# Final layer norm of a mixture-of-experts layer: token lists for each expert group, one tile per expert unit

## The chip, the cores and the metric

The kernel runs on one core of a Trainium2 chip. The metric is the device time of one execution in microseconds (us). The core has five engines with their own instruction queues: TensorE (PE, matmuls), VectorE (DVE), ScalarE (ACT), GpSimd (POOL) and SyncE (SP, which here only starts DMAs). Each engine runs its instructions in order; they wait for each other through semaphores. POOL also starts all indirect DMAs, those that gather or scatter rows by an index list.

## The reference, cut to what matters

```python
x = layer_norm(ALPHA * x + fourier_mixer(x), ln_g[0], ln_b[0])      # h, (4096, 1024) float32
scores = sigmoid(x @ w_router)                                      # 32 experts in 4 groups of 8
sel = scores + b_router
group = argmax(sum of the two highest sel of each group)            # one group per token
experts = the two highest sel inside that group
gate = scores[experts] / sum
y[t] = sum_k gate[t, k] * (silu(x[t] @ w_gate[e]) * (x[t] @ w_up[e])) @ w_down[e]
out = layer_norm(ALPHA * x + y, ln_g[1], ln_b[1])
```

Both experts of a token lie in the same group. So the sum of a token is complete when the last expert of its group is done.

## The kernel before, in words

The first stage is a two-step Fourier transform and two projections; it ends with the first layer norm, whose rows h are stored twice in DRAM: in h_rows, from which the experts gather, and in sums (`acc`), into which they add. The norm is invariant to scale, so ALPHA is divided out of the gates and the epsilon. Beside it the router runs for 256 tokens a group of steps (`choose`, `take_ranks`, `place`): it ranks every token within its experts by matmuls with a triangular matrix, keeps the counts in `base`, and POOL writes an entry (token, gate) of 8 bytes for each of the two experts into `lists` (`list_tokens`, L1543, four indirect DMAs). An expert's list is laid out over 64 lanes.

The expert stage runs over units: 320 entries of one expert. A unit with more than 256 entries is wide, else narrow. The number of units and which expert and rows each has come from a table `utab` that DVE works out from the counts between L1370 and L1400. With the inputs of the reference there are 33 units. All matmuls are float32 made of three passes over a high and a low part. In a unit (the functions `unit` of each engine)

- SP loads twelve pieces of weights of 512 KB, four each of gate, up and down (`load_piece`, L566), into six slots. A slot is free when DVE has split what was in it. Ahead of piece 4 it waits for `ent_ok` and loads the list entries of the next unit.
- ACT rounds each piece to its high part, DVE subtracts to get the low part (`split`, L1056 and L1356).
- TensorE runs four blocks of gate products, then four of up products in two banks (`first_products`, L880): block k of the up products from the third on needs `hid_ok` of block k - 2. Then four blocks of down products (`down`, L893) with the transposes of the next unit's rows between them, and in a wide unit the third product `down_c`.
- ACT applies silu to the gate blocks. For each block k DVE multiplies (hid), ACT rounds it (hidT high), DVE subtracts (hidT low).
- ACT and DVE each scale half of the y rows; POOL adds them to `sums` by indirect DMA with addition (`scatter`), the second tile only after the first has landed. In a wide unit a third scatter follows.
- POOL also gathers the rows of the unit after the next, waits for all of it, and copies the entries one step on (`ent_now`, `ent_next`).

DVE's order in unit u is: four splits of down pieces of u; for each k the split of piece k of u + 1 (k < 3), hid(k) and the low part; two transposed tiles; hidC; splits and tiles of u + 1 with the two y halves between them. ACT's order follows the same pattern. POOL's iteration u begins with the wait for the first y rows of u, as its scatters, gathers and waits for u - 1 have come first.

The final stage begins when POOL has seen the last scatter land (`moe_done`). It goes over 32 tiles of 128 consecutive rows in eight buffers: SP loads, DVE takes the statistics (`statistics`, L1213) and inverts, ACT takes the root and normalises, DVE multiplies by the gain, POOL adds the shift (L1687), SP stores.

## Time and profile before

| | us |
|---|---|
| median of 3 runs | 2350.23 (2346.81 to 2350.3) |
| the profiled execution | 2350.37 |
| its span, first to last instruction | 2348.4 |
| expert stage, first gate product of the first unit to that of the last | 860.6 to 2173.6 |
| from the landing of the last scatter to the end | 2219.0 to 2348.4 |

The page has the busy time and share of each engine, a timeline in 40 slices, and the costliest groups of instructions. A row of the timeline names the start, the duration, the engine, the line, the operation, and output<-input by the program's names; in brackets stands how long the engine sat idle before it and what released it. TensorE's clock has two levels, 1.2 and 2.4 GHz; the profile gives the granted one as 0.5 and 1.

### The profile page before, as it was taken

To read this page: it belongs to the slowest core of one execution; us is meant where nothing else is said; L and a number is where in the kernel's file an instruction comes from. 1 tells how busy PE (TensorE), PEld (TensorE's weight loads), DVE (VectorE), ACT (ScalarE), POOL (GpSimd) and SP (SyncE) were. 2 spreads that over 40 slices of the span, in tenths; PEclk is the share of its full clock that TensorE was granted. 3 is DMA by queue.
4 is the path that set the end of the run, shared out by engine and by line. 5 is a ranking of instruction groups with operands and counts; after the bars stand their busy time and mean duration, and the time that the engine had idled before them with its cause. 6 is when DMAs were issued, how large, how long until landed. Compare 5 with 4: busy or idle time off the path is not lost.

```text
span 2348.4 us, 37687 instructions
## 1 busy us (share of the span) xinstructions
PE 2127.3 (91%) x12222; PEld 1801.6 (77%) x12223; DVE 1373.1 (58%) x2254; ACT 998.2 (43%) x1442; POOL 582.7 (25%) x493
## 2 busy tenths in 40 slices
PE   8999899999999449999999999999999999999600
PEld 3443678888888349999999999999999999998500
DVE  3321148888887746555655656555555565555298
ACT  1221123333233226555555645655455565554143
POOL 1000034444544411211121121212111121211166
PEclk9999999999999769999999999999999999999855
DMA  6880233443333347767776866877677777766376
GB/s 226 283 287 21 67 126 113 147 147 125 116 127 108 126 153 210 222 203 195 219 216 184 248 194 211 227 223 197 180 220 218 219 218 228 209 202 183 98 286 238
DMA packets 136067, 435.59 MB, mean 185 GB/s; under 512 B 30912, under 2 KB 35008, under 8 KB 131904
## 3 DMA queue, kind: packets, MB, share of 16 engines
q1 hardware_dynamic: 98592, 307.12, 38.6%
q0 software_dynamic: 37440, 128.01, 21.6%
q8 instruction: 21, 0.34, 0.1%
q14 instruction: 14, 0.11, 0.0%
HBM read 328.01 MB, written 108.10 MB: 186 GB/s over the span
## 4 chain that ended last, share of the span: by engine, by line
PE 90%; POOL 3%; issue 3%; DMA 2%; DVE 2%; ACT 0%; SPq 0%; POOLq 0%; ACTq 0%; DVEq 0%
PE ps L877 36%; PE ps L901 15%; PE ps L759 15%; PE ps L696 5%; POOL fin_r L1689 3%; PE ps L865 3%; PE ps L741 3%; PE ps L909 2%; PE ps L715 2%; PE ps L793 2%; PE ps L650 1%; PE ps L780 1%; PE ps L700 1%; PE ps L870 1%; PE ps L659 1%
## 5 line engine op out<-in xcount | busy, mean ns | idle before, releaser
L901 PE MATMUL ps<-wd_hi,hidT 128*128 128x512 f32 x1056 | 293.0, 402 | 0.4 <-ACT hidT L1099 0.4
L1359 DVE TENSOR_TENSOR wd_lo<-wraw,wd_hi 128x1024 fp32r<-128x1024 f32 x132 | 161.9, 1226 | 199.0 <-ACT wd_hi L1057 198.7
L901 PEld LDWEIGHTS ps<-wd_hi,hidT 128*128 128x128 f32 x1056 | 190.1, 189 | 36.3 <-ACT hidT L1099 0.8
L1359 DVE TENSOR_TENSOR wg_lo<-wraw,wg_hi 128x1024 fp32r<-128x1024 f32 x132 | 161.4, 1224 | 92.6 <-ACT wg_hi L1057 92.5
L1632 POOL DMA_INDIRECT sums<-yrow_a,ent_now x33 | 57.2, 1733 | 558.4 <-DVE yrow_a L1422 515.4
L1359 DVE TENSOR_TENSOR wu_lo<-wraw,wu_hi 128x1024 fp32r<-128x1024 f32 x132 | 160.7, 1218 | 52.0 <-ACT wu_hi L1057 51.9
L877 PE MATMUL ps<-mxT_hi,wg_hi 128*128 128x256 f32 (+1 forms) x1056 | 163.3, 297 | 13.4 <-issue 13.4
L1099 ACT CAST hidT<-hid 128x320 fp32r<-128x320 f32 x132 | 60.7, 460 | 257.3 <-DVE hid L1440 257.3
L877 PEld LDWEIGHTS ps<-mxT_hi,wg_hi 128*128 128x128 f32 x1056 | 149.7, 191 | 17.9 <-issue 16.0
L877 PE MATMUL ps<-mxT_lo,wg_hi 128*128 128x256 f32 (+1 forms) x1056 | 163.2, 297 | 0.0
L877 PE MATMUL ps<-mxT_hi,wg_lo 128*128 128x256 f32 (+1 forms) x1056 | 162.6, 297 | 0.0
L877 PE MATMUL ps<-mxT_hi,wu_lo 128*128 128x256 f32 (+1 forms) x1056 | 162.0, 296 | 0.0
L877 PE MATMUL ps<-mxT_hi,wu_hi 128*128 128x256 f32 (+1 forms) x1056 | 161.8, 296 | 0.0
L877 PE MATMUL ps<-mxT_lo,wu_hi 128*128 128x256 f32 (+1 forms) x1056 | 161.8, 296 | 0.0
L1057 ACT CAST wu_hi<-wraw 128x1024 fp32r<-128x1024 f32 x132 | 135.8, 1054 | 36.6 <-DMA wraw<-expert_w_up 31.8
L877 PEld LDWEIGHTS ps<-mxT_lo,wg_hi 128*128 128x128 f32 x1056 | 149.3, 192 | 0.0
L877 PEld LDWEIGHTS ps<-mxT_hi,wg_lo 128*128 128x128 f32 x1056 | 148.7, 191 | 0.0
L877 PEld LDWEIGHTS ps<-mxT_lo,wu_hi 128*128 128x128 f32 x1056 | 147.9, 190 | 0.0
L877 PEld LDWEIGHTS ps<-mxT_hi,wu_hi 128*128 128x128 f32 x1056 | 147.9, 190 | 0.0
L877 PEld LDWEIGHTS ps<-mxT_hi,wu_lo 128*128 128x128 f32 x1056 | 147.9, 190 | 0.0
L1005 ACT CAST xt_hi<-ps 128x256 fp32r<-128x256 f32 x128 | 41.4, 375 | 246.9 <-PE ps L741 246.9
L901 PE MATMUL ps<-wd_lo,hidT 128*128 128x512 f32 x528 | 142.3, 391 | 0.0
(212 smaller groups left out, 4120.0 us busy)
## 6 DMA issues: line engine op xcount, KB each, us to landing
wraw<-expert_w_gate SPq DMA_DIRECT2D x132, 512.0 KB, 5.4
wraw<-expert_w_up SPq DMA_DIRECT2D x132, 512.0 KB, 5.4
wraw<-expert_w_down SPq DMA_DIRECT2D x132, 512.0 KB, 4.4
xch<-x SPq DMA_DIRECT2D x16, 1024.0 KB, 6.7
first_stage<-ych SPq DMA_DIRECT2D x16, 1024.0 KB, 8.3
yt<-first_stage SPq DMA_DIRECT2D x16, 1024.0 KB, 4.9
fin_r<-sums SPq DMA_DIRECT2D x32, 512.0 KB, 3.9
out<-fin_r SPq DMA_DIRECT2D x32, 512.0 KB, 2.9
```

The source lines that it names most:

```text
L696: mm = nc.tensor.matmul(dst, foldT[:, m, g, c * P:(c + 1) * P], T[:, m, g, h * HALF:(h + 1) * HALF], start=(g == 0), stop=(m == 1 and g == ...
L715: nc.tensor.matmul(bank[s1_bank(n)], f1, xch[:, b, n % 4 // 2, n % 2 * HALF:(n % 2 + 1) * HALF], start=True, stop=True).then_inc(job_ps, 1)
L741: mm = nc.tensor.matmul(s2_bank(jj)[:, lo:lo + P], yt[:, b, q, cc * P:(cc + 1) * P], m2t[:, b, q, :], start=True, stop=True)
L759: mm = nc.tensor.matmul(ps[:, cols], xt[l][:, m, c, :], w[r][:, c, cols], start=(n == 0 and c == 0 and not edge_row), stop=(n == 2 and c = ...
L865: mm = nc.tensor.transpose(psT[k % 2][:, lo:lo + P], xrow_s[t][:, c, :], ident)
L877: mm = nc.tensor.matmul(ps[k % 2][:, 0:n], w[l][:, c, k * P:(k + 1) * P], mxT[r][:, c, 0:n], start=(i == c == 0), stop=(i == 2 and c == CH ...
L901: mm = nc.tensor.matmul(psY[h], hidT[:, l, c, t * P:(t + 1) * P], wd[r][:, c, cols], start=(i == c == 0), stop=(i == 2 and c == FC - 1))
L1057: nc.scalar.copy(piece(0, j), wraw[:, j % SLOTS, :]).then_inc(whi_ok, 1)
L1099: nc.scalar.copy(hidT[:, 0, k, :], hid[:, k % 2, :]).then_inc(hh_ev, 1)
L1359: nc.vector.tensor_tensor(piece(1, j), wraw[:, j % SLOTS, :], piece(0, j).bitcast(F32), ALU.subtract).then_inc(wlo_ok, 1)
L1632: pool.indirect_dma_start(acc, bass.IndirectOffsetOnAxis(ap=ent_now[0:n, t, 0:1], axis=0), yrow[t], None, compute_op=ALU.add).then_inc(don ...
L1689: nc.gpsimd.tensor_tensor(fin_r[:, b, :], fin_r[:, b, :], lnb2, ALU.add).then_inc(fh_ok, 1)
```

## The change

The final normalisation is spread over the expert stage.

- Each of the 4 expert groups gets a token list too. `LISTS` is 36; a list is now linear, 35 x 128 entries, so that lanes and their bit operations go. A third entry per token (without a gate) is written by `list_tokens`: six indirect DMAs instead of four. The padding entries of the expert lists point to 512 spare rows of `sums` and `h_rows`, which are filled from x (before: 128); those of the group lists to real tokens.
- `ln_table` on DVE, with one turn over TensorE, works out `ltab`: for each unit u which tile of 128 tokens it normalises, among those whose group was finished before u, one new one a unit. Where none is ready, the unit repeats the last (at first tile 0, whose sums are not final; it is done again later). It also has the start of each tile in the lists and the number of batches of ten that remain.
- In unit u POOL first gathers the tile's rows from `sums` (`ln_gather`), DVE, ACT, DVE normalise them at the places shown below, and POOL scatters them to `out` between its two y scatters (`ln_store`). At the end of its iteration POOL waits for that store. SP waits for it ahead of loading the next tile's token numbers, which come between weight pieces 9 and 10.
- After the units the remaining tiles are done in batches of ten (`FB`), gathered and scattered by POOL; the shift moves from POOL to DVE. Each store waits until the one before it has landed.
- The entries of a unit are loaded by three DMAs instead of four; the gain and shift vectors are loaded ahead of the expert stage.

The diff, cut to its core:

```diff
-UROWS = UNIT // LANES
-LROWS = 2 * S // LANES
-USED_ROWS = S // LANES + 2
+LISTS = E + EG
+CAP = 35 * P
+FILL = 512
 STARTS = -(-S // UNIT)
-LANE_BITS = LANES.bit_length() - 1
-LIST_BITS = (E * LROWS).bit_length() - 1
 MAX_UNITS = 2 * S // UNIT + E
 SLOTS = 6
 PIECES, GU_PIECES = 12, 8
-FB = 8
+FB = 10
...
-            sp.wait_ge(pad_made, 1)
-            sp.dma_start(lists.rearrange("(p e r) w -> p e (r w)", p=LANES, e=E)[:, :, 0:2 * USED_ROWS],
-                         bass.AP(padl.tensor, padl.offset,
-                                 [list(padl.ap[0]), [0, E], [1, 2 * USED_ROWS]])).then_inc(pad_out, 16)
-            sp.dma_start(acc[S:S + P, :], x[0:P, :]).then_inc(pad_out, 16)
-            sp.dma_start(hd[S:S + P, :], x[0:P, :]).then_inc(pad_out, 16)
+            sp.wait_ge(pad_made, 4)
+            lists_pad = lists.rearrange("(e p r) w -> p e (r w)", p=P, e=LISTS)
+            for pad, lo, hi in ((padl[0], 0, E), (padl[1], E, LISTS)):
+                sp.dma_start(lists_pad[:, lo:hi, :],
+                             bass.AP(pad.tensor, pad.offset,
+                                     [list(pad.ap[0]), [0, hi - lo], [1, 2 * CAP // P]])).then_inc(pad_out, 16)
+            sp.dma_start(acc[S:S + FILL, :], x[0:FILL, :]).then_inc(pad_out, 16)
+            sp.dma_start(hd[S:S + FILL, :], x[0:FILL, :]).then_inc(pad_out, 16)
...
+            sp.dma_start(lng2, bcast(ln_g[1], P)).then_inc(ln2_in, 16)
+            sp.dma_start(lnb2, bcast(ln_b[1], P)).then_inc(ln2_in, 16)
+            sp.wait_ge(ltab_ok, 1)
+            own_wait(sp, glist_out, 32 * GROUPS, sp_gate)
+            load_ln_tile(ln_slot(0))
...
+                    if j == 9:
+
+                        tile = ln_slot(u)
+                        own_wait(sp, lrow_out, 16 * u, sp_gate)
+                        load_ln_tile(tile)
...
+            first_tile = sp.value_load(ltab[:, LANES + LN_COLS + 1:LANES + LN_COLS + 2], min_val=0, max_val=MAX_LN)
+            with sp.Fori(0, batches(sp)) as i:
+                own_wait(sp, batch_ok, i + 1, sp_gate)
                 for b in range(FB):
...
+                    start = ln_start(sp, first_tile + FB * i + b)
+                    sp.dma_start(lents[:, b, :], lists[ds(start, P), :]).then_inc(lents_in, 16)
+            own_wait(sp, batch_ok, batches(sp) + 1, sp_gate)
...
+            def ln_deviation(u):
+                act.wait_ge(lvar_ok, u + 1)
+                nc.scalar.activation(lnstd[:, 0:1], lnmv[:, 0, 1:2], ACT.Sqrt, bias=eps2_c).then_inc(lstd_ok, 1)
+
+            def ln_normal(u):
+                act.wait_ge(lsh_ok, u + 1)
+                nc.scalar.activation(lnrow, lnrow, ACT.Identity, bias=lnsh[:, 0:1], scale=lnrs[:, 0:1]
+                                     ).then_inc(lnorm_ok, 1)
...
                         split(u + 1, k)
                     act.wait_ge(hid_ok, 4 * u + k + 1)
                     nc.scalar.copy(hidT[:, 0, k, :], hid[:, k % 2, :]).then_inc(hh_ev, 1)
+                    if k == 0:
+                        ln_deviation(u)
+                    if k == 1:
+                        ln_normal(u)
...
+            def ln_table():
+                link(nc.vector.tensor_scalar(gti, base[:, E:LISTS], float(P - 1), None, ALU.add))
+                link(nc.vector.tensor_scalar(gti, gti, P.bit_length() - 1, None, ALU.logical_shift_right))
+                nc.vector.tensor_scalar(lim, base[:, E:LISTS], float(-P), 0.0, ALU.add, ALU.max)
+                link(nc.vector.tensor_copy(tiles, gti))
+                nc.vector.tensor_scalar(ends, ucum.rearrange("p (g j) -> p g j", j=EPG)[:, :, EPG - 1], unit_c,
+                                        None, ALU.is_le)
+                link(nc.vector.tensor_tensor_scan(upto, tiles, zer[:, 0:EG], 0.0, ALU.add, ALU.add))
+                link(nc.vector.tensor_tensor(ends, ends, tiles, ALU.mult))
+                link(nc.vector.tensor_tensor(past, upto, tiles, ALU.subtract))
+                nc.vector.tensor_reduce(lcol[:, 0:1], ends, AX, ALU.add)
+                nc.vector.tensor_scalar(lcol[:, 2:3], upto[:, EG - 1:EG], -1.0, unit_c, ALU.add, ALU.min)
...
+                nc.vector.tensor_reduce(lcol[:, 1:2], pick, AX, ALU.add).then_inc(lcol_made, 1)
+                dve.wait_ge(ltab_ps, 1)
+                done, last_u, steps_f, more_f = lrow_f
+                link(nc.vector.tensor_tensor_scan(done, ones[0:1, 0:LANES], psLtab[:, 0:LANES], 0.0,
+                                                  ALU.add, ALU.min))
...
+            LN_STEPS = 2
+
+            def ln_statistics(u):
+                dve.wait_ge(lrow_in, 16 * u + 16)
+                step.begin(unit_steps + LN_STEPS * u)
+                statistics(lnrow, 0).then_inc(lvar_ok, 1)
+
+            def ln_invert(u):
+                dve.wait_ge(lstd_ok, u + 1)
+                link(nc.vector.reciprocal(lnrs[:, 0:1], lnstd[:, 0:1]))
+                nc.vector.scalar_tensor_tensor(lnsh[:, 0:1], lnmv[:, 0, 0:1], -1.0, lnrs[:, 0:1],
+                                               ALU.mult, ALU.mult).then_inc(lsh_ok, 1)
+
+            def ln_gain(u):
+                dve.wait_ge(lnorm_ok, u + 1)
+                nc.vector.tensor_tensor(lnrow, lnrow, lng2, ALU.mult).then_inc(lgain_ok, 1)
+
+            def ln_shift(u):
+                dve.wait_ge(lgain_ok, u + 1)
+                nc.vector.tensor_tensor(lnrow, lnrow, lnb2, ALU.add).then_inc(lfin_ok, 1)
+
             def unit(u, more):
                 wide = unit_wide(dve, u)
                 for k in range(FC):
                     split(u, GU_PIECES + k)
+                ln_statistics(u)
                 for k in range(FC):
                     if more and k < FC - 1:
                         split(u + 1, k)
+                    if k == 1:
+                        ln_invert(u)
+                    if k == 3:
+                        ln_gain(u)
                     dve.wait_ge(u_ps, 4 * u + k + 1)
                     dve.wait_ge(silu_ok, 4 * u + k + 1)
                     nc.vector.tensor_tensor(hid[:, k % 2, :], sgate[:, k, :], psU[k % 2][:, 0:UNIT],
@@ -1445,6 +1549,7 @@
                 if more:
                     turn_x(u + 1, 0)
                     turn_x(u + 1, 1)
+                ln_shift(u)
...
+                nc.vector.tensor_tensor(fin_r[:, b, :], fin_r[:, b, :], lng2, ALU.mult).then_inc(fb_ok, 1)
+                dve.wait_ge(fb_ok, t + 1)
+                nc.vector.tensor_tensor(fin_r[:, b, :], fin_r[:, b, :], lnb2, ALU.add).then_inc(fh_ok, 1)
+
+            with dve.Fori(0, batches(dve)) as i:
+                for b in range(FB + 2):
+                    if b < FB:
+                        normal(FB * i + b, i, b)
+                    if 0 < b <= FB:
+                        invert(FB * i + b - 1, (b - 1) % LB)
+                    if b >= 2:
+                        gain(FB * i + b - 2, b - 2)
...
-                for s in range(2):
-                    for k in range(2):
+                for k in range(3):
+                    for s in range(2):
+                        j = 3 * s + k
                         pool.indirect_dma_start(
-                            lists, bass.IndirectOffsetOnAxis(ap=desti[:, 2 * s + k:2 * s + k + 1], axis=0),
-                            payg[:, 4 * s + 2 * k:4 * s + 2 * k + 2], None).then_inc(list_out, 16)
+                            lists, bass.IndirectOffsetOnAxis(ap=desti[:, j:j + 1], axis=0),
+                            payg[:, 2 * j:2 * j + 2], None).then_inc(list_out if k < 2 else glist_out, 16)

             def shift(g, b):
...
+            def ln_gather(u):
+                own_wait(pool, lent_in, 16 * u + 16, pool_gate)
+                pool.indirect_dma_start(lnrow, None, acc, bass.IndirectOffsetOnAxis(ap=lent[:, 0:1], axis=0)
+                                        ).then_inc(lrow_in, 16)
+
+            def ln_store(u):
+                own_wait(pool, lfin_ok, u + 1, pool_gate)
+                pool.indirect_dma_start(out, bass.IndirectOffsetOnAxis(ap=lent[:, 0:1], axis=0), lnrow, None
+                                        ).then_inc(lrow_out, 16)
+
             def unit(u, ahead):
                 wide = unit_wide(pool, u)
+                ln_gather(u)
                 for t in range(2):
                     pool.wait_ge(ya_ok, 2 * u + t + 3)
                     own_wait(pool, yd_ok, 2 * u + t + 3, pool_gate)
                     if t:
                         own_wait(pool, y_out, 32 * u + 16, pool_gate)
                     scatter(t, P, y_out)
+                    if t == 0:
+                        ln_store(u)
                 if ahead == 2:
                     turned(u + 1)
                     gather(u + 2)
...
+                own_wait(pool, lrow_out, 16 * u + 16, pool_gate)
...
+            with pool.Fori(0, batches(pool)) as i:
+                own_wait(pool, lents_in, 16 * FB * i + 16 * FB, pool_gate)
                 for b in range(FB):
-                    fin(FB * i + b, b)
+                    pool.indirect_dma_start(fin_r[:, b, :], None, acc,
+                                            bass.IndirectOffsetOnAxis(ap=lents[:, b, 0:1], axis=0)
+                                            ).then_inc(fin_in[b], 16)
+                for b in range(FB):
+                    if b:
+                        own_wait(pool, fin_out, 16 * FB * i + 16 * b, pool_gate)
+                    own_wait(pool, fh_ok, FB * i + b + 1, pool_gate)
+                    pool.indirect_dma_start(out, bass.IndirectOffsetOnAxis(ap=lents[:, b, 0:1], axis=0),
+                                            fin_r[:, b, :], None).then_inc(fin_out, 16)
+                own_wait(pool, fin_out, 16 * FB * i + 16 * FB, batch_ok)
```

## Rows read from the trace of the kernel before

**Rows 1.** The page, busy us of each engine, share of the span, instructions.

```profile
PE 2127.3 (91%) x12222; PEld 1801.6 (77%) x12223; DVE 1373.1 (58%) x2254; ACT 998.2 (43%) x1442; POOL 582.7 (25%) x493
```

**Rows 2.** Windows: us, busy PE, PEld, DVE, ACT, POOL; clock, DMA share, GB/s.

```profile
860.60:2173.60 1313.00, 1309.73 (x8576) 1228.03 (x8576) 750.97 (x912) 711.86 (x974) 239.05 (x220) 1.00 0.72 209
1470.51:1506.36 35.85, 35.85 (x259) 33.85 (x258) 22.27 (x28) 21.42 (x30) 6.75 (x6) 1.00 0.78 234
2219.30:2348.40 129.10, 0.00 (x0) 0.00 (x0) 111.14 (x192) 48.97 (x64) 74.98 (x32) 0.50 0.74 268
```

**Rows 3.** DMA issues of POOL: count, median us from issue to landing.

```profile
xrow_a<-h_rows,ent_in POOLq DMA_INDIRECT x33, 8.0
...
sums<-yrow_a,ent_now POOLq DMA_INDIRECT x33, 8.3
...
rows<-x,rowg POOLq DMA_INDIRECT x32, 5.0
h_rows<-rows,rowg POOLq DMA_INDIRECT x32, 3.8
```

**Rows 4.** Timeline of the final stage: start, us, engine, line, operation.

```profile
2240.88 0.29 ACT L1139 ACTIVATE lnstd<-lnmv,eps_c 128x1 f32<-128x1 f32 x1 [1.44 <-DVE lnmv L1218]
...
2242.80 0.68 DVE L1215 BATCH_NORM_STATS2 lnst<-fin_r 128x6 f32<-128x512 f32 x1
2242.95 2.35 POOL L1689 TENSOR_TENSOR fin_r<-fin_r,lnb 128x1024 f32<-128x1024 f32 x1 [1.23 <-DVE fin_r L1495]
...
2244.22 0.21 DVE L1218 BATCH_NORM_AGGREGATE lnmv<-lnst 128x2 f32<-128x12 f32 x1
...
2245.24 1.21 DVE L1495 TENSOR_TENSOR fin_r<-fin_r,lng 128x1024 f32<-128x1024 f32 x1
2245.35 1.24 ACT L1144 ACTIVATE fin_r<-fin_r,lnsh,lnrs 128x1024 f32<-128x1024 f32 x1 [0.60 <-DVE lnsh L1484]
```

**Rows 5.** Timeline of POOL around two narrow units, and of SP.

```profile
1466.23 1.75 POOL L1632 DMA_INDIRECT sums<-yrow_a,ent_now  x1 [13.90 <-DVE yrow_a L1422]
1475.29 1.56 POOL L1632 DMA_INDIRECT sums<-yrow_b,ent_now  x1 [7.31 <-DMA sums<-yrow_a,ent_now]
...
1487.27 0.91 POOL L1661 COPY ent_next<-ent_in 128x6 int32<-128x6 int32 x1 [2.28 <-DMA xrow_b<-h_rows,ent_in]
...
1525.30 0.19 POOL L1661 COPY ent_next<-ent_in 128x6 int32<-128x6 int32 x1 [4.71 <-DMA xrow_c<-h_rows,ent_in]
...
1488.42 1.46 SPq L561 DMA_DIRECT2D ent_in<-expert_lists  x2
```

**Rows 6.** Chain in order of time: gate and up products of units.

```profile
1470.51 23.04 PE ps L877 x192
...
1952.20 28.16 PE ps L877 x192
```

**Rows 7.** Timeline of DVE, then ACT, in the narrow unit from 1470.51.

```profile
1484.94 0.49 DVE L1440 TENSOR_TENSOR hid<-sgate,ps 128x320 f32<-128x320 f32 x1 [0.25 <-PE ps L877]
...
1486.90 1.23 DVE L1359 TENSOR_TENSOR wg_lo<-wraw,wg_hi 128x1024 fp32r<-128x1024 f32 x1 [0.46 <-ACT wg_hi L1057]
1488.05 0.48 DVE L1440 TENSOR_TENSOR hid<-sgate,ps 128x320 f32<-128x320 f32 x1
...
1471.19 1.28 ACT L1057 ACT_TABLE_LOAD   x1 [0.40 <-issue]
1472.48 1.05 ACT L1057 CAST wd_hi<-wraw 128x1024 fp32r<-128x1024 f32 x1
...
1494.11 0.46 ACT L1099 CAST hidT<-hid 128x320 fp32r<-128x320 f32 x1 [1.04 <-DVE hid L1440]
```

**Rows 8.** Timeline of PE, first matmuls of the expert stage.

```profile
860.61 2.07 PE L877 MATMUL ps<-mxT_hi,wg_hi 128*128 128x256 f32 x8 [10.08 <-issue]
```

**Rows 9.** Chain in order of time: the last unit's scatters.

```profile
2206.19 6.04 DMA sums<-yrow_a,ent_now
...
2213.01 5.97 DMA sums<-yrow_b,ent_now
```

More of the change, by code:

```diff
@@ L240, in trunk_kernel @@
         ucol = at("ucol", 152.5, 8)
+        gt = [at(f"gt{i}", 156 + i / 32, EG) for i in range(7)]
+        gti = at("gti", 156.5, EG, I32)
+        lcol = at("lcol", 156.75, 4)
+        lrow_f = [at(f"lrow_f{i}", 157 + i / 4, LANES)[0:1, :] for i in range(4)]
         grow = Row(192, 200)
@@ L852, in _ @@
             mm.then_inc(utab_ps, 1)
+            pe.wait_ge(lcol_made, 1)
+            for k in range(2):
+                mm = nc.tensor.matmul(psLtab[:, k * P:(k + 1) * P], lcol[:, k:k + 1], ident,
+                                      start=True, stop=True)
+            mm.then_inc(ltab_ps, 1)
             pe.sem_inc(y1_ps, 2)
```

238 lines of the change are left out of this document (121 added, 117 removed).

## Prediction

> **What bounds the kernel now.** I read the page's engine shares first [rows 1]: TensorE is busy 91% of the span; VectorE (DVE), ScalarE (ACT) and GpSimd (POOL) are at 58, 43 and 25%. The table by stage [rows 2] then shows two regimes. In the expert stage (860.6 to 2173.6 us, 32 units, 41.03 us each) TensorE runs all but without a gap at full clock, 35.85 us for a narrow unit. The final normalisation, from 2219.3 on, has no TensorE work at all. So 129 us of tail are to be won, and every microsecond that the new work adds to a unit is paid 32 times. The third view is the order on each engine inside one unit [rows 5 to 7], because every engine takes its instructions strictly in order.
>
> **How much leaves the tail.** The routing follows from the reference's inputs alone: the four groups hold 992, 1017, 1033 and 1054 tokens, 8+8+9+9 = 34 tiles of 128 rows, and there are 33 units (as many scatters in [rows 3]), 16 of them wide. The first eight units repeat tile 0, the other 25 do one tile each, 9 remain: one batch of 10. In the tail now a tile costs 3.57 us, POOL's shift of 2.35 and DVE's gain of 1.21 in turn [rows 4]. Afterwards, from the landing of the last scatter: ten list loads, which SP issues at 0.73 each [rows 5], and about 2 to land, 9.3; first gather, with its issue, 5.4: 14.7; then on DVE three statistics at 1.65, two inverts at 0.35, one gain and one shift at 1.21 before the first tile is out, 23. Then 4.45 a tile (1.65 + 0.35 + 2.42), the last two without statistics, 60; a last store of 5, in all 65. The stores are a serial chain too: with the 3.8 us of the h_rows stores [rows 3] plus issue it keeps up with DVE, with the 8.3 of the scatters the tail would take 109. I take 65, because these are plain writes like the first. Before, this stretch took 2348.4 - 2219.0 = 129.4 [rows 9]. **Gain 64**, at worst 20.
>
> **What it costs in a unit: DVE waits for a gather that is sent late.** The new statistics stand on DVE between the four splits of the down weights and the first hidden product, hid(0), and wait for the row gather of the same unit. That gather is the first instruction of POOL's iteration. Where is POOL then? The narrow unit starts on TensorE at 1470.51 [rows 6]. POOL sends the previous unit's first scatter at 1466.23 and its second when that has landed, at 1475.29; the gathers for a later unit follow, and the iteration ends with the copy of ent_next at 1487.27, 16.8 us into the unit; the next one at 1525.30 is 18.9 into its unit [rows 5]. These are the last two of eleven units read this way, 16.1 to 19.0, mean 17.6. But hid(0) was due at 1484.94, +14.4 [rows 7]. So the new gather is sent after the product that it now holds up.
> The landing L of that gather: 17.6, + 0.7 because the scatters come later relative to the next unit (below), + 0.8 for copy, semaphores and loop, + the gather itself. Its price lies between 5.0 (rows from x, little else in flight) and 8.0 (xrow_a) [rows 3]; I take 6.5, because weight loads go out at the same time, though fewer than beside xrow_a. L = 25.6 us after the unit's start. From L: statistics 1.65 [rows 4], the split behind them 1.2 and hid(0) 0.49 [rows 7]: it ends at H0 = 28.9.
> TensorE needs hid(0) out of the bank for its third up product, at +17.3 in a narrow unit (three quarters of the 23.04 us [rows 6]): it stands for 11.6 us, in a wide one for 7.7. What is late next, counted from H0 with the durations of [rows 4, 7]: ACT casts hid (0.5), loads the square root's table (1.28), takes the root (0.29) and casts a weight (1.05), 3.0; DVE splits it, inverts and forms hid(1), 5.1 (3.1 in the trace). ACT cast 0.5, normalisation 1.24, weight cast, DVE split and hid(2), 9.4. ACT cast, DVE low half, gain 1.21, hid(3), 12.05; its cast, 12.6. The down products need that. From the same cast to the next unit's start it was 11.8 (1494.57 [rows 7] to 1506.36 [rows 2]), less 0.6 for matmuls that are already done: the next unit starts at H0 + 23.8. The shift (1.21) ahead of hidC hides behind the down products; but the first y rows are ready only 4.5 instead of 5.1 before the next unit, which is the 0.7 above.
> A narrow unit thus takes 28.9 + 23.8 = 52.7, +16.85. Wide ones, half of the units, lose less: their longer gate and up products (28.16 against 23.04 [rows 6]) hide in the wait, 2.56 on average. (16.85 - 2.56) x 32 = **457**. In the first unit POOL has nothing ahead of the gather and is early, so only the longer chain counts, about 3 instead of 17: -14. The last unit, to its first scatter: +9.
>
> **TensorE's clock.** After the stop of 10.08 us ahead of the stage the first eight matmuls ran at 1.2 GHz and took 2.07 us [rows 8]; later eight of them take 0.96 (23.04 / 24). Each unit now has such a stop and a shorter one ahead of the down products. The slow stretch after the first lies inside the chain to hid(1), that after the second may not. I take 1 us a unit, +33; bounds 0 and 3, that is 0 and +99.
> The Trainium skill, "TensorE: Matmul & The Clock Gate", section "Why this matters for your kernels", asks for no idle gaps over about 3 us between bursts of matmuls, or the clock falls to half. The row agrees; by that rule both stops of every unit would be punished, which is rival (c).
>
> **The table load.** In the trace a load takes 1.28 and the next cast starts right behind it [rows 7]; that is what I counted. The Trainium skill, "ScalarE: Activation LUTs", section "What ACT_TABLE_LOAD costs", gives 1.38 us of draining beside it. By that another 1.4 x 33 = 46 us would be lost; the rows show no such gap, and they decide.
>
> **The rest.** DMA: a gather and a store of 0.5 MB each join a narrow unit whose DMA engines are 78% busy [rows 2], but the unit gets half as long again, so no bound there. POOL's store goes out while POOL waits for its first scatter: nothing. SP now waits for that store ahead of down pieces 10 and 11, which come about 11 us into the unit instead of before it; queued behind are the next unit's gate weights, which DVE wants only after L. The stop itself hides this; without it, it would cost 2 to 4 us a unit. List tables: about 35 linked operations of 0.2 [rows 4] and a turn over TensorE, 8 us, most of it in DVE's idle time ahead of the first transposes: +3, bounds 0 and +10. First stage: 3.3 MB more to fill, 12 us at the tail's 268 GB/s [rows 2], in a queue ahead of loads of x: +4, bounds 0 and +15. Routing: two more small list DMAs per group on POOL, which is not the bound, and one DVE step fewer: 0, bounds -5 and +10.
> Sum: 2350.4 (the profiled execution; its span is 2348.4, the median of the runs shown 2350.2) + 457 - 14 + 9 + 33 + 3 + 4 - 64 = 2778, **about 2780**.
>
> **Rivals.** (a) The latencies fall, because the unit is longer. The last unit shows undisturbed scatters: 6.8 us to the second and 6.0 to land [rows 9], instead of 9.1 and some 9. POOL would be 3.3 earlier and the gather take 5.0: 32 x 4.8 = 154 less, 2626. For it: the queues are quiet while all engines wait; against: the delayed pieces and four gate pieces now go out beside these very scatters.
> (b) The wait is covered and only the order costs. If the gather landed by +11, hid(0) would be in time; but 23.8 behind it instead of 21 costs a narrow unit 3 and a wide one about 1: +65 + 7 - 64, 2358. POOL would have to be 14 us earlier than in all eleven units.
> (c) Both stops halve the clock: the down products of every unit partly at 1.2 GHz, 3 us a unit instead of 1: 2846.
> (d) The other side: the gather is covered and the chain fits beside TensorE's products, so that the tail's gain is left: 2350 + 7 - 64 = 2293. One point decides: whether DVE's wait ahead of hid(0) ends before +11. POOL's rows speak against it.
>
> **How the numbers follow.** Forecast 0.66; (a) 0.16; (c) 0.10; (b) 0.03; (d) 0.05. The forecast's own bounds (gather -48 or +48, clock -33 or +66, tail stores up to +44, the rest up to +28) make 2690 to 2880. With (a) and (c) the range is 2610 to 2900; (b), (d) and the far ends are left out. A measurement of this kernel tells about 0.2% from no change: faster 0.05, that is (d); same 0.01, where (b) ends nearer to the old time than worked out; slower 0.94.
>
> **What would show it.** TensorE's waits in the stage, all but none now: afterwards ahead of the up products and of the first down products, some 10 and 3 us a unit, released by DVE's hid and ACT's hidT. DVE's statistics released by the DMA of the row gather after 8 to 12 us. That gather issued 18 to 20 us into the unit. Narrow units near 53 us. One batch, a tail of 60 to 70. It is wrong if the gather is issued before +5, or if DVE waits under 2 us.

## Result, and the profile after

The changed kernel takes 2791.6 us (median of 4 runs, 2786.1 to 2804.7), the kernel before 2350.3 beside it: a ratio of 1.189, 95% interval 1.184 to 1.194. It is 19% slower. The profiled execution took 2795.3 us, its span 2793.2.

The page of the changed kernel answers [rows 1]: TensorE has the same work and is busy 80% instead of 91%.

```profile
PE 2237.6 (80%) x12226; PEld 1878.9 (67%) x12227; DVE 1423.7 (51%) x2383; ACT 1058.1 (38%) x1497; POOL 622.5 (22%) x580
...
PE 33%; DMA 32%; issue 13%; DVE 10%; ACT 7%; POOLq 2%; POOL 1%; SPq 0%; DVEq 0%; ACTq 0%
PE ps L774 13%; DMA lnrow<-sums,lent 8%; DMA sums<-yrow_a,ent_now 7%; DMA sums<-yrow_c,ent_now 5%; DMA xrow_c<-h_rows,ent_in 5%; PE ps L921 4%; PE ps L711 4%; DMA sums<-yrow_b,ent_now 4%; DVE hid L1544 2%; PE ps L756 2%; ACT wg_hi L1077 2%; PE ps L730 2%; PE ps L808 2%; ACT hidT L1128 2%; DMA xrow_b<-h_rows,ent_in 2%
```

The last two lines are the chain that ended last, by engine and by line. DMA is on it for 32% of the span: the row gather, and ahead of it the scatters and token gathers behind which POOL sends it.

The windows of the changed kernel (us, busy PE, PEld, DVE, ACT, POOL; clock, DMA share, GB/s) answer [rows 2]: 32 units; the last unit, up to just before SP's first list load; the rest. The last scatter itself landed at 2715.5 (sent at 2709.56, 5.98 us to land).

```profile
866.44:2670.35 1803.91, 1419.27 (x8576) 1306.61 (x8577) 867.95 (x1136) 804.15 (x1071) 298.38 (x284) 0.89 0.57 170
2670.35:2716.70 46.35, 34.84 (x240) 31.98 (x240) 13.66 (x22) 11.30 (x18) 7.36 (x6) 0.92 0.37 84
2716.70:2793.20 76.50, 0.00 (x0) 0.00 (x0) 39.74 (x70) 14.68 (x20) 20.04 (x20) 0.50 0.37 137
```

The stage grew from 1313.0 to 1803.9 us, 41.03 to 56.37 a unit, while the DMA engines fell from 72 to 57% busy: their bandwidth over the stage is not what bounds it. From the landing of the last scatter to the end it is 77.7 us instead of 129.4.

The waits (engine, line, releaser: us in total, times, longest):

```profile
DVE lnst L1249 <- DMA lnrow<-sums,lent: 379.4, 32, 15.6
...
PE ps L897 <- DVE hid L1544: 319.5, 39, 15.7
...
POOL sums L1732 <- DMA sums<-yrow_a,ent_now: 127.3, 30, 4.8
...
PE ps L921 <- ACT hidT L1128: 58.3, 44, 2.1
```

One narrow unit of the changed kernel, which starts at 2055.97, in the timelines of POOL, DVE, ACT and PE (start, us, engine, line, operation, idle before):

```profile
2055.36 1.60 POOL L1732 DMA_INDIRECT sums<-yrow_b,ent_now  x1 [3.91 <-DMA sums<-yrow_a,ent_now]
...
2072.76 0.19 POOL L1775 COPY ent_next<-ent_in 128x6 int32<-128x6 int32 x1 [1.05 <-issue]
2074.77 0.98 POOL L1741 DMA_INDIRECT lnrow<-sums,lent  x1 [1.82 <-issue]
...
2081.35 0.69 DVE L1249 BATCH_NORM_STATS2 lnst<-lnrow 128x6 f32<-128x512 f32 x1 [13.16 <-DMA lnrow<-sums,lent]
...
2084.07 0.48 DVE L1544 TENSOR_TENSOR hid<-sgate,ps 128x320 f32<-128x320 f32 x1
...
2085.06 1.28 ACT L1103 ACT_TABLE_LOAD   x1
...
2089.11 0.49 DVE L1544 TENSOR_TENSOR hid<-sgate,ps 128x320 f32<-128x320 f32 x1
...
2084.60 2.08 PE L897 MATMUL ps<-mxT_hi,wu_hi 128*128 128x256 f32 x8 [11.11 <-DVE hid L1544]
```

The gather leaves 18.8 us into the unit and has landed at +25.4, where the statistics begin; hid(0) starts at +28.1 instead of +14.4 [rows 7], and TensorE stood 11.1 us for it. At 52.3 us this is one of the shorter narrow units; in the mean of them the gather leaves at +20.1 and hid(0) starts at +29.8, against +14.6 before.

### The profile page after: what moved, and what is told of

The parts are those of the page before. It is cut to its first block, busy times and chain, and to the rows that moved or that the text cites. A ratio compares the mean times of both kernels' runs of the same rounds, so it can differ in the third digit from the quotient of the medians.

```text
span 2793.2 us, 38440 instructions
## 1 busy us (share of the span) xinstructions
PE 2237.6 (80%) x12226; PEld 1878.9 (67%) x12227; DVE 1423.7 (51%) x2383; ACT 1058.1 (38%) x1497; POOL 622.5 (22%) x580
## 4 chain that ended last, share of the span: by engine, by line
PE 33%; DMA 32%; issue 13%; DVE 10%; ACT 7%; POOLq 2%; POOL 1%; SPq 0%; DVEq 0%; ACTq 0%
PE ps L774 13%; DMA lnrow<-sums,lent 8%; DMA sums<-yrow_a,ent_now 7%; DMA sums<-yrow_c,ent_now 5%; DMA xrow_c<-h_rows,ent_in 5%; PE ps L921 4%; PE ps L711 4%; DMA sums<-yrow_b,ent_now 4%; DVE hid L1544 2%; PE ps L756 2%; ACT wg_hi L1077 2%; PE ps L730 2%; PE ps L808 2%; ACT hidT L1128 2%; DMA xrow_b<-h_rows,ent_in 2%
## 5 line engine op out<-in xcount | busy, mean ns | idle before, releaser
L897 PE MATMUL ps<-mxT_hi,wu_hi 128*128 128x256 f32 (+1 forms) x1056 | 197.5, 338 | 319.5 <-DVE hid L1544 319.5
L897 PEld LDWEIGHTS ps<-mxT_hi,wu_hi 128*128 128x128 f32 x1056 | 174.7, 224 | 329.1 <-DVE hid L1544 328.8
L921 PE MATMUL ps<-wd_hi,hidT 128*128 128x512 f32 x1056 | 318.9, 422 | 58.3 <-ACT hidT L1128 58.3
L921 PEld LDWEIGHTS ps<-wd_hi,hidT 128*128 128x128 f32 x1056 | 199.8, 198 | 113.1 <-ACT hidT L1128 76.5
L1249 DVE BATCH_NORM_STATS2 lnst<-lnrow 128x6 f32<-128x512 f32 x33 | 22.9, 694 | 379.4 <-DMA lnrow<-sums,lent 379.4
L897 PE MATMUL ps<-mxT_lo,wu_hi 128*128 128x256 f32 (+1 forms) x1056 | 186.2, 326 | 0.0
L897 PE MATMUL ps<-mxT_hi,wg_hi 128*128 128x256 f32 (+1 forms) x1056 | 164.6, 299 | 19.3 <-issue 14.7
L897 PEld LDWEIGHTS ps<-mxT_lo,wu_hi 128*128 128x128 f32 x1056 | 173.3, 220 | 0.0
L897 PE MATMUL ps<-mxT_hi,wu_lo 128*128 128x256 f32 (+1 forms) x1056 | 170.3, 306 | 0.0
L1077 ACT CAST wd_hi<-wraw 128x1024 fp32r<-128x1024 f32 x132 | 138.0, 1045 | 83.4 <-DMA wraw<-expert_w_down 82.5
L897 PEld LDWEIGHTS ps<-mxT_hi,wu_lo 128*128 128x128 f32 x1056 | 158.3, 203 | 0.0
## 6 DMA issues: line engine op xcount, KB each, us to landing
w_in_s<-fourier_w_in SPq DMA_DIRECT2D x1, 4096.0 KB, 21.8
```

Of the source, the lines that this page charges most:

```text
L897: mm = nc.tensor.matmul(ps[k % 2][:, 0:n], w[l][:, c, k * P:(k + 1) * P], mxT[r][:, c, 0:n], start=(i == c == 0), stop=(i == 2 and c == CH ...
L921: mm = nc.tensor.matmul(psY[h], hidT[:, l, c, t * P:(t + 1) * P], wd[r][:, c, cols], start=(i == c == 0), stop=(i == 2 and c == FC - 1))
L1077: nc.scalar.copy(piece(0, j), wraw[:, j % SLOTS, :]).then_inc(whi_ok, 1)
```

## The experiments

Two theories stood at the start. Mine: the late gather holds hid(0), and every microsecond of its lateness is paid. The rival: any steps put into that place of the unit cost that much, whatever the gather does. "Stage" below is the time from the first unit's start to the last one's, 1313.0 before and 1803.9 after; N and W are mean lengths of the 15 narrow and 16 wide units behind the first (36.47 and 45.53 before, 55.63 and 57.78 after).

### No gather in the units

```
 def ln_gather(u):
     own_wait(pool, lent_in, 16 * u + 16, pool_gate)
-    pool.indirect_dma_start(lnrow, None, acc, ...).then_inc(lrow_in, 16)   # once, ahead of the loop
```

> The changed kernel with one edit: the row gather of the normalisation is sent once, ahead of the units, and not in any unit. The units still load the list, normalise the row buffer and store it, in the same order. Left out is only the data: the rows that the units normalise are always those of the first gather. My theory: DVE's wait for the gather is what costs; without it the product hid(0) is due as before at about +14, the longer chain behind it (23.8 instead of 21 us) is all that is left, at most 3 us in a narrow unit and 1 in a wide one, and SP's late down pieces some 0 to 2 more. 2350 + 8 (tables, lists) - 53 (tail as measured) + 0 to 65, so 2305 to 2400, likeliest 2340. Rival, order: if the position of the new steps on DVE and ACT, and not the gather, makes the loss, it stays near 2790. Rival, list load and store: if SP's wait for the store is a chain of its own, 2450 to 2600.

Measured: 2434.1 us, ratio to before 1.035 (1.032 to 1.037); stage 1439.6, N 42.87, W 47.11. So the gather is 364 of the 491 us of the stage, and the rival is out. But what is left is 127 us, not the 65 at most that I had allowed. Of a narrow unit's 6.4 us, 3.3 lie behind hid(0) (25.2 us from its start to the next unit, 21.8 before; forecast 2.8), and 3.1 ahead of it, where I had nothing. ACT's timeline of this kernel shows one part of the reason, in a unit that starts at 1359.50:

```profile
1369.11 1.05 ACT L1077 CAST wd_hi<-wraw 128x1024 fp32r<-128x1024 f32 x1 [3.21 <-DMA wraw<-expert_w_down]
...
1373.59 1.05 ACT L1077 CAST wd_hi<-wraw 128x1024 fp32r<-128x1024 f32 x1 [3.10 <-DMA wraw<-expert_w_down]
```

The last two down pieces are late, because SP waits for the row store before it sends them.

### No gather, and the list load behind the last piece

```
-        if j == 9:                       # SP, load_unit
-            own_wait(sp, lrow_out, 16 * u, sp_gate); load_ln_tile(tile)
+    own_wait(sp, lrow_out, 16 * u, sp_gate); load_ln_tile(tile)   # after j = 11
...
+    act.wait_ge(entc_ok, u + 1)          # ACT, ahead of ln_normal's activation
```

> The kernel of k1_no_gather (gather sent once, ahead of the units; only data left out) with one edit more: SP's list load and its wait for the previous unit's row store stand behind the last piece of the down weights instead of ahead of the last two (and ACT's normalisation waits for the copy of ent_now, which keeps the order of store and next write). In k1_no_gather hid(0) starts at +17.7 in narrow units, against 14.6 in the kernel before, and SP issues the last two down pieces 4 to 5 us into the unit. My theory: these late pieces are that delay; without them hid(0) is back near +14.9 in the 15 narrow units, 0.3 earlier in the wide ones: 2434 - 15 x 2.8 - 16 x 0.3 = 2387, bounds 2375 to 2400. Rival: the three splits and the statistics on DVE cost it themselves (statistics 1.65 us), then the time stays between 2415 and 2434.

Measured: 2410.6 us (ratio 1.026, 1.024 to 1.027), 24 less, half of what I expected and outside the bounds of both theories; 18 of the 24 lie in the stage. N 41.97, W 46.86. The late pieces are about a third of the 3.1 us ahead of hid(0), which still starts at +16.6. What the rest is, these two runs don't separate; the statistics and the split behind them stand there.

### The same edit on the complete changed kernel

Here SP's lines alone are moved, with the gather in its place; ACT's added wait is not in it.

> The changed kernel, complete, with one edit: SP's list load and its wait for the row store behind the last down piece. The same edit took 24 us from the kernel without the gather (2434 to 2411). My theory, as forecast: with the gather the stop of DVE hides the late pieces, so nothing changes, 2792 with bounds 2780 to 2800. Rival: the pieces are late for a second reason and the same 24 us come back, 2768.

Measured: 2838.9 us (ratio 1.208, 1.206 to 1.210), 47 *more*. Neither theory had that sign. The waits of this kernel:

```profile
POOL sums L1730 <- DMA sums<-yrow_a,ent_now: 194.4, 32, 7.2
```

POOL waits 6.1 us for its first scatter to land instead of 4.2. The two pieces that SP had held back until the row store was done now go out beside the scatter and the store: on average 1.5 us before and 0.4 us behind the issue of the first scatter, against 9.4 and 10.0 us behind it in the changed kernel. All of POOL's chain moves by that: the gather leaves 1.7 us later into a unit (21.9 and 21.0 against 20.1 and 19.3), and the units are 1.5 and 1.7 longer. The pair without the gather shows the same slowing, off the chain, where it costs nothing. Median us from the issue of this scatter to its landing, without the edit and with it:

```profile
sums<-yrow_a,ent_now POOLq DMA_INDIRECT x33, 6.4
```

```profile
sums<-yrow_a,ent_now POOLq DMA_INDIRECT x33, 8.7
```

So the edit slows the first scatter by about 2 us in both pairs. Where a trace gives it, it is 6.4 to 6.5 in the five kernels that hold the pieces back, and 8.0 to 8.8 in the eight that don't, the kernel before among them [rows 3]. That this is a collision of transfers is argued from the order of issue; no run changed the traffic alone.

### The gather one step earlier

```
     own_wait(pool, entc_ok, u + 2, pool_gate)
+    ln_gather(u + 1)
     ...gathered(u + 2); copy of ent_next...      # ln_gather(u) is gone from the top
```

> The changed kernel, complete, with the row gather sent one step earlier on POOL: right behind the copy of ent_now of the previous iteration, ahead of POOL's wait for the token rows of the unit after next. In the changed kernel's trace 3.2 to 11.8 us lie between that copy and the gather, 209.6 us over 32 units. My theory (every microsecond by which the gather leaves earlier is won in full): 2792 - 210 = 2582, or up to 60 more if the gather takes longer because it then runs beside the gathers of token rows (10 us instead of 6.6), so 2580 to 2650. Rival: if the next thing behind DVE is close (late down pieces, list load), less than half comes back, above 2690.

Measured: 2621.3 us (ratio 1.114, 1.111 to 1.118), 170 less, inside what my theory gave. The gather leaves 5.5 us earlier in a unit, hid(0) starts 5.4 earlier, and a unit is 5.7 (N) and 5.3 (W) shorter: a slope of one.

### No square root in the units

```
-nc.scalar.activation(lnstd[:, 0:1], lnmv[:, 0, 1:2], ACT.Sqrt, bias=eps2_c)
+nc.scalar.activation(lnstd[:, 0:1], lnmv[:, 0, 1:2], ACT.Identity, bias=eps2_c)
```

> The changed kernel with the square root in the units replaced by a plain copy with the same operands, so the units normalise with the variance itself instead of its root (a wrong scale, the same work otherwise), and ACT loads no table in the middle of the unit. My theory: one table load of 1.28 us per unit lies on the chain hid(0), cast, root, inversion, hid(1), so 33 x 1.28 = 42 us less: 2750, bounds 2740 to 2765. Rival, the price that the page on the activation tables of the Trainium skill gives (a load with draining, 2.66): 88 us less, 2704. Rival: hidden, no change.

Measured: 2727.6 us (ratio 1.159, 1.156 to 1.163), 64 less: 1.93 us a unit, more than my bounds and less than the first rival. hid(1) comes 1.41 us nearer to hid(0) (3.64 instead of 5.05), which is the load of 1.28 and little more, so there is no room for a price of 2.66 in the chain. Most of the rest goes with TensorE's clock. The windows from hid(3) to the next unit in the same narrow unit of both kernels (us, busy PE, clock, DMA share, GB/s), the changed kernel first:

```profile
2315.54:2329.46 13.92, 12.90 (x53) 0.88 0.28 62
```

```profile
2260.26:2272.62 12.36, 11.42 (x54) 1.00 0.29 67
```

In the changed kernel 14 of these 31 stretches (10 N, 4 W) have a granted clock of 0.87 to 0.91 and are some 1.57 us longer than those at 1.00; without the root none has. Before them TensorE had stood about 11 us for hid(0), had worked partly at the lower level, 1.2 GHz, and had then stood up to 2.1 us again for hidT (58.3 us in all; 24.3 without the root). 31 x 1.41 + 14 x 1.57 makes 66, against 63 measured behind hid(0) in these 31 units. The whole stage is 62 shorter, which agrees only because two other things nearly cancel: hid(0) itself comes 0.5 later in the narrow units (8 us in all), and the first unit is 6.1 shorter, where TensorE had stood 4.6 us for a weight split at its end. Why one unit has the slow stretch and another not, these runs don't show; all six kernels here with the chain of 5.05 have 5 to 14 of them, the kernel before and the one without the root none (of the other orders below, at 3.11, three have two).

### TensorE kept busy in the stop

```
 for k in range(FC):                      # up products
+    if k == 2:                           # 84 (narrow) or 56 (wide)
+        pe.wait_ge(silu_ok, 4 * u + 3)
+        for r in range(84): nc.tensor.matmul(psG[0][:, 0:NARROW], mxT[0][:, 0, 0:P], mxT[0][:, 1, 0:NARROW], ...)
```

> The changed kernel, complete, with filling work on TensorE: while it waits for hid(0) it does 84 (narrow) or 56 (wide) matmuls of 128x256 at about 0.12 us each into a free PSUM bank, 10.1 or 6.7 us of the 11 to 12 and 8 to 9 us that it waits. So the stop ahead of the third up product is nearly gone and the clock should stay at the higher level. My theory (clock term 1 us a unit): 33 us less than 2792, that is 2759, bounds 2730 to 2785. Rival, both stops of a unit count: 3 us a unit, 2695. Rival: the slow stretch behind the stop is off the chain, no change or, where the filling work overruns the stop, up to 20 us more.

Measured: 2809.5 us (ratio 1.196, 1.193 to 1.198), 18 more, where my theory wanted 33 less; by the total the last rival is right. In the profiled execution (2801.0) two things lie behind that: in the first and the last unit there is no such stop, and the filling work itself delays them, by 5.5 and some 17 us. From the start of the second unit to that of the last it is 1746.9 against 1758.8, 12 us less; the mean clock rose from 0.898 to 0.952, and 5 instead of 14 stretches behind hid(3) are slow, 9 x 1.57 = 14. The slow matmuls right behind the stop (2.08 us for eight, above) cost nothing themselves: the chain to hid(1) takes 5.05 us either way. By this count the clock's price is the 14 stretches, 22 us. It rests on one execution: the other three took 6 to 13 us longer, at a mean clock of 0.945 to 0.947, so in the medians little or nothing of the 12 us is left.

### All tiles at the end

```
-ln_statistics(u), ln_invert(u), ln_gain(u), ln_shift(u), ln_deviation(u), ln_normal(u)
-ln_gather(u), ln_store(u), load_ln_tile(tile)          # and the waits for them
-more_f[:, 2:3] = more_f[:, 3:4] - more_f[:, 1:2]       # tiles left = all - done
+more_f[:, 2:3] = more_f[:, 3:4] - zer[0:1, 0:1]
```

> The changed kernel, complete, with no normalisation in the units: all 34 tiles go in four batches of ten behind the last unit (some tiles twice). My theory: the units fall back to 41.03 us each, so all the loss of the stage is in the inserted steps and nothing in the lists, the constants or the larger first stage; these leave +6. Each batch costs what the one batch takes in the changed kernel, some 73 us from the last landing, so 4 x 73 = 292 instead of 129: 2350 + 6 + 163 = 2519, bounds 2490 to 2540. Rival: if the linear lists themselves (one load of 256 rows instead of two halves) or the fuller memory disturb the units, each unit is over 41.5 us and the time over 2540.

Measured: 2521.7 us (ratio 1.073, 1.072 to 1.075). N 36.47, W 45.51, stage 1312.9: the lists and the fuller first stage cost the units nothing, and four batches cost what was worked out.

### Other orders: is the idea to be had at all?

> A complete kernel that tries the idea with another order: a unit normalises the rows that were gathered in the unit before. POOL stores the finished rows and gathers the next tile at the top of its iteration, ahead of its wait for the first y rows; DVE's four steps and ACT's two stand between the splits of the down weights and the SiLU products, ahead of hid(0), where both engines wait for TensorE; the list entries are copied, so that SP waits for that copy and not for the store. My theory (only the late gather, the longer chain behind hid(0) and the late pieces cost, and all three are gone): units of 41 to 41.5 us, tail gain of 53 kept, 2350 + 6 - 53 + 0 to 16 = 2303 to 2319. Rival, traffic: a narrow unit in which the DMA engines are already 78% busy gets 1 MB more, or POOL's longer serial chain (store, gather, two scatters, token rows) becomes the bound in narrow units: 2 to 5 us in 15 units, 2335 to 2395. Rival, that any such step in the unit costs 2 us or more on each: over 2370.

The core of the edit:

```
 def unit(u, ahead):                      # POOL
+    ln_store(u); own_wait(pool, lrow_out, 16 * u + 16, pool_gate)
+    if ahead: ln_gather(u + 1); own_wait(pool, lrow_in, 16 * u + 32, pool_gate)
 ...
 def unit(u, more):                       # DVE
+    ln_statistics(u); split; split; ln_invert(u); split; ln_gain(u); split; ln_shift(u)
```

Measured: 2344.1 us, ratio 0.997 (0.996 to 0.999). The steps in the unit cost little when their rows are there (hid(0) starts 1.1 us later in a narrow unit, 0.4 in a wide one): TensorE's 320 us of waiting for hid are gone. But N is 38.96 and W 45.91, so 44 of the 52 us that the tail gives are lost again. POOL's store and gather stand there in series with its scatters, one of the rivals named. The next kernel hid them behind POOL's other waits:

```
-                ln_store(u); ...; ln_gather(u + 1)      # top of POOL's iteration
                 gather(u + 2); gather_c(u + 2)
+                if ahead: ln_store(u + 1)
                 own_wait(pool, y_out, ...); ...; copy of ent_now
+                own_wait(pool, lrow_out, ...); ln_gather(u + 2)
                 gathered(u + 2); copy of ent_next
```

> Complete. The kernel of k6_lagged with POOL's serial chain shortened: the finished rows are stored behind the issue of the token row gathers, while POOL waits for its second scatter to land, and the next tile is gathered right behind the copy of ent_now, while POOL waits for the token rows. In k6_lagged the store and the gather, 7.0 and 6 to 8 us from issue to landing, stood alone in POOL's order; its narrow units took 38.96 us (41 to 42 in the later ones of a row of narrow units) against 36.47 before, its wide ones 45.91 against 45.53. My theory: POOL's chain was that loss, so narrow units fall to 36.5 to 37.2 and the time to 2344 - 33 = 2311, bounds 2300 to 2322. Rival: the loss is the additional traffic (1 MB a unit), which is the same here; then it stays between 2335 and 2345.

Measured: 2353.1 us, ratio 1.002 (1.001 to 1.003): slower than the one it should have mended, N 39.58. "POOL's serial chain" as I had put it is wrong; what matters is one point of it. ACT's waits for up pieces in the stretch 890 to 2120, in the kernel before, then this one, then the last kernel below:

```profile
ACT wu_hi L1057 <- DMA wraw<-expert_w_up: 9.9, 9, 1.7
```

```profile
ACT wu_hi L1080 <- DMA wraw<-expert_w_up: 74.9, 25, 6.0
```

```profile
ACT wu_hi L1079 <- DMA wraw<-expert_w_up: 6.1, 10, 1.2
```

SP waits for the copy of ent_next before it loads the next entries, and the up pieces of the next unit are queued behind that. The copy came at +18.0 (N) before, at +21.9 in the kernel ahead of this one, and comes at +24.5 here. First the lists of the final batch alone:

```
 with sp.Fori(0, batches(sp)) as i:
-    own_wait(sp, batch_ok, i + 1, sp_gate)
     ...the ten list loads...
+    own_wait(sp, batch_ok, i + 2, sp_gate)
```

> Complete. The kernel of k8_lagged_early with the ten list loads of the tail issued as soon as SP has nothing left to load, instead of after the last scatter has landed. In the changed kernel's trace these ten loads take 11.3 us to issue and some 2 to land on the path of the tail. My theory: 11 to 13 us less than k8_lagged_early, near 2299. Rival: POOL or DVE is not ready earlier, under 4 us.

Measured: 2338.8 us (0.995, 0.994 to 0.997), 14 less. Then the wait and the gather behind the copy:

```
-                own_wait(pool, lrow_out, ...); ln_gather(u + 2)
                 gathered(u + 2); copy of ent_next
+                own_wait(pool, lrow_out, ...); ln_gather(u + 2)
```

> Complete. The kernel of k9_lists_ahead with POOL's wait for the row store and the next row gather moved behind the copy of ent_next. In k8_lagged_early and k9_lists_ahead that copy comes at +24.5 instead of +18.0 into a unit; SP waits for it ahead of the entry loads, the four up pieces of the next unit stand behind these on SP, and ACT waited 80 us in the stage for up pieces (10 in the kernel before, 64 in k6_lagged). My theory: this chain (copy of ent_next, SP, up pieces, ACT, y products) is what both lagged kernels lose in narrow units; with the copy back at +18 to +20 the narrow units fall from 39.5 to 36.5 to 37.3 and the time to 2339 - 40 = 2299, bounds 2290 to 2312. Rival, traffic: the loss comes from 1 MB more in a narrow unit and stays, 2330 to 2340.

Measured: 2321.2 us (0.987, 0.986 to 0.989): the right direction, 18 instead of 40, with the copy at +21.2 and N 38.33. In iterations of wide units POOL waited ahead of the store, with the third scatter behind it; the store was moved behind that:

```profile
1242.66 0.98 POOL L1716 DMA_INDIRECT xrow_b<-h_rows,ent_in  x1 [0.30 <-issue]
1254.98 0.98 POOL L1750 DMA_INDIRECT out<-lnrow,rowix  x1 [11.34 <-issue]
1256.27 1.48 POOL L1734 DMA_INDIRECT sums<-yrow_c,ent_now  x1 [0.30 <-issue]
```

```
-                if ahead: ln_store(u + 1)
                 own_wait(pool, y_out, 32 * u + 32, pool_gate)
                 with pool.If(wide > 0): ...; scatter(2, LANES, yc_out)
+                if ahead: ln_store(u + 1)
```

> Complete. The kernel of k10_lists_first with the store of the finished rows moved on POOL behind the issue of the third scatter (in narrow units behind the landing of the second). In k10_lists_first POOL waits in front of this store until DVE's last step at about +14 into the unit, 11.3 us at 1243.6 us of its trace, with the third scatter of the previous wide unit queued behind it, and ent_next is copied at +23 to +24 there, against +16 to +17 before. My theory: the copy comes at +18 to +19 everywhere and the up pieces are in time: the 15 narrow units fall from 38.33 to 36.6 to 37.3, 2321 - 20 = 2301, bounds 2294 to 2310. Rival: traffic, the time stays over 2315.

Measured: **2307.5 us, ratio 0.982 (0.981 to 0.984)**, 1.8% faster than the kernel before. The copy is at +18.8, N 37.51, W 45.75. Over the four kernels N follows the copy: 38.96, 39.58, 38.33 and 37.51 with the copy at +21.9, +24.5, +21.2 and +18.8. The last one's windows from the first to the last unit, and the rest:

```profile
862.93:2195.93 1333.00, 1317.13 (x8576) 1230.17 (x8577) 878.92 (x1138) 799.26 (x1071) 334.54 (x316) 1.00 0.78 232
2195.93:2307.10 111.17, 35.99 (x240) 33.39 (x240) 52.99 (x90) 27.07 (x39) 27.14 (x25) 0.67 0.36 115
```

The DMA engines are now 78% busy instead of 72 [rows 2] and the stage is only 20 us longer: traffic, the rival in several of these runs, is at most those 20, and the 1.0 us by which a narrow unit is still longer lies ahead of hid(0) (+15.7 against +14.6), where the six new steps stand.

## Why the prediction was right

The forecast was 2780 us in a range of 2610 to 2900; 2791.6 was measured. By the terms of the sum, against the profiled execution:

| term | forecast | measured |
|---|---|---|
| 32 units, clock and first unit in them (457 + 33 - 14) | +476 | +490.9 |
| last unit, start to landing of the last scatter | +9 | -0.2 |
| first stage and tables (start of first unit 860.6, then 866.4) | +7 | +5.8 |
| tail, from the last landing | -64 | -51.7 |

The forecast terms make 2778, the measured ones 2795 of 2795.3. The +5.8 is itself uncertain: in the kernels with the same first stage the first unit starts between 862.2 and 868.4. The stated bounds don't add up in one way: the lower one, 2690, is the plain sum of its terms, while the upper ones (48 + 66 + 44 + 28) make 2966 by the same sum and not 2880. The result does not depend on it.

**The mechanism** was as forecast: gather issued at +19.7 on average (19.1), landing after 6.6 us (6.5), statistics waiting 11.9 us for it (8 to 12), hid(1) 5.05 behind hid(0) (5.1), TensorE waiting 319.5 us for hid, 10 a unit (10). Three of the named signs were off in size: narrow units 55.6 (52.7 + 1), the wait for hidT 58.3 us, 1.8 a unit (3), and the tail 77.7 (60 to 70). Removing the gather, and moving it, showed it by experiment with a slope of one.

**L** was 0.9 us short: from the copy of ent_next to the gather it takes 2.0 us, not the 0.8 that I had estimated; the copy itself came 0.6 earlier than forecast, at +17.7. Rival (a) was half there: the first scatter landed after 6.5 us instead of 8.3, but the token gathers, between it and the copy, took 8.3 to 10.7 instead of 8.0 to 9.2 (medians). The quicker scatter goes with SP's late pieces and not with the longer unit, as the same edit in two pairs of kernels shows. That so little was missing from L is in part luck: the quicker scatter and the slower token gathers and loop, none of them forecast, nearly cancel.

**The order.** 23.8 us behind the end of hid(0) were forecast for a narrow unit; they were 25.3, of which about 1 is clock.

**The clock** was a term of 33 and is worth 22 by the count of slow stretches. The place was half right: the slow stretch behind the long stop, which I put on the chain, is off it, and the one behind the second, "may not", is where the cost arises, in 14 of 31 units. Rival (c), every unit by 3 us, is out. The rule against idle gaps over about 3 us between bursts of matmuls (the Trainium skill, "TensorE: Matmul & The Clock Gate", section "Why this matters for your kernels") agrees with the trace in that the stretch behind the long stop, from hid(0) to hid(3), has a granted clock of 0.79 on average; it does not say which of the slow stretches costs time. The second stop, at most 2.1 us, is under the page's figure, and behind it 14 stretches have 0.87 to 0.91 all the same; whether that stop or the long one ahead of it is the cause, no run here separates.

**The table load.** The rows' 1.28 held in the chain (1.41 measured with all that goes with it), and the Trainium skill's 2.66 ("ScalarE: Activation LUTs", section "What ACT_TABLE_LOAD costs") did not. Its effect on the total, 64, was larger than my expectation of 42; what goes beyond the chain went with slow stretches that were gone and with a shorter first unit.

**SP's wait.** "The stop itself hides this; without it, it would cost 2 to 4 us a unit" had the wrong frame. Without the stop it cost 0.55 a unit (18 of the 24 us); with the stop, the wait was worth 47 us: with it the first scatter, which is on the chain, lands some 2 us sooner. I had named what was queued behind that wait, not what it held off.

**The last unit** cost nothing: POOL has little left to do there, the gather leaves at +10.9, and hid(0) starts at +17.3 against 16.2. This is the cover that rival (d) asked for, in one unit of 33.

**The tail** gained 52, not 64; this is the term that was furthest off for its size. Ten list loads took 11.3 us to issue instead of 7.3, so POOL sent the first gather 14.9 us after the landing (9.3 forecast) and DVE had rows after 19.2 (14.7 forecast). DVE made up for part of it, at 4.2 us a tile (4.45 forecast), and was done after 61.9 (60 forecast). But the stores did not keep up, as the forecast had assumed. The second tile and the last one, on DVE and then on POOL:

```profile
2746.13 1.23 DVE L1605 TENSOR_TENSOR fin_r<-fin_r,lnb 128x1024 f32<-128x1024 f32 x1
...
2776.19 1.23 DVE L1605 TENSOR_TENSOR fin_r<-fin_r,lnb 128x1024 f32<-128x1024 f32 x1
...
2750.56 1.82 POOL L1809 DMA_INDIRECT out<-fin_r,lents  x1 [5.53 <-DMA out<-fin_r,lents]
...
2786.41 0.95 POOL L1809 DMA_INDIRECT out<-fin_r,lents  x1 [3.32 <-DMA out<-fin_r,lents]
```

The second tile was ready 3.2 us before its store was sent, the last one 9.0 us: from the second on, each store left 1.0 to 1.7 us behind the landing of the one before, 4.7 us apart on average. The forecast had named this chain, with a bound of +44, but its point estimate took nothing for it; these 9 us are most of the miss.

**Rival (b)**, 2358, was priced too low: the kernel without the gather, which is its case, took 2434. The 65 us of order were 127 of order and late pieces, and its tail was as much too short as that of the forecast.

## What to carry to other kernels

When work for idle slots needs data that another queue sends, find first at which moment of the iteration that queue can send it; if that is after the slot, fetch one iteration ahead, or the wait is paid once per iteration at slope one. Then look for the point in the slower queue for which others wait (here one small copy, with SP and the weight pieces behind it), and put the additional transfers behind that point, not merely into that engine's waits. A wait that looks harmless can also be what keeps a transfer from colliding with one on the chain. Test its removal on the complete kernel too; on the reduced one the same slowing was off the chain and didn't show in the time.

## What the runs showed of the hardware

With two weight pieces of 512 KB sent earlier in each unit, POOL's wait for the scatter beside them was 1.9 us longer, though the DMA engines were not 60% busy over the stage. The granted clock behind a stop of 2.1 us or less, with a stop of about 11 us before it, was at its full level in 17 stretches and between 0.87 and 0.91 in 14 others of the same kernel, and no run shows what separates them; with 1.4 us less in the chain before, all 31 were at the full level. So a small edit can win or lose more than its own duration.
